# The second projections of both feed-forward stages: token tiles 0 and 2 by seven products per pair of k blocks, then tiles 1 and 3 as they were

## The reference, cut to what matters

```python
def _sqrelu_mlp(h, w1, w2):                 # h: 512 x 1024, w1: 1024 x 4096, w2: 4096 x 1024
    return jnp.square(jax.nn.relu(h @ w1)) @ w2
...
    for i in range(DEPTH_2):                # DEPTH_2 = 2
        ...                                 # attention, its residual sum and layer norm
        h = x * (1.0 + sc_c) + sh_c
        y = _sqrelu_mlp(h, mlp_w1[i], mlp_w2[i])
        x = _layer_norm(DN_ALPHA * x + (1.0 + g_c) * y, ln_g[i, 1], ln_b[i, 1])
```

## Time and profile before

| | |
|---|---|
| median of the runs | 3385.03 us |
| profiled execution, its own time | 3387.39 us |
| its span in the trace | 3385.8 us |
| mean granted TensorE clock | 0.97 |
| TensorE matmul busy | 3185.5 us (94%), 12406 records |
| VectorE busy | 1596.7 us (47%) |
| ScalarE, GpSimd busy | 563.2 us (17%), 250.1 us (7%) |
| HBM traffic, mean | 162 GB/s |
| first feed-forward stage, down projection | 2410.9 to 2633.5 us |
| second one | 3152.5 to 3372.4 us |

### The profile page before, as it was taken

The page is one execution under the profiler, slowest core; times in us unless marked ns, Lnnn a source line. Parts: engine busy times, 40 slices in busy tenths (PEclk is TensorE's granted clock), DMA queues, the critical chain, the costliest instruction groups (busy, mean ns, idle before and its releaser), DMA issues. The chain is left out here.

```text
span 3385.8 us, 38571 instructions
## 1 busy us (share of the span) xinstructions
PE 3185.5 (94%) x12406; PEld 1748.5 (52%) x12407; DVE 1596.7 (47%) x3615; ACT 563.2 (17%) x1280; POOL 250.1 (7%) x377
## 2 busy tenths in 40 slices
PE   7999999999989888979998998999999899899998
PEld 3446767744437433323333544488644566488543
DVE  6546576567656533324443577565202333465103
ACT  1002222210002111111221315310000233100000
POOL 1010000011110211112222100000000000000000
PEclk9999999999989899999999998999999999899999
DMA  7562121368762598997996611022121223022210
GB/s 236 169 199 63 38 75 38 88 210 260 245 215 102 206 362 338 360 362 289 358 346 218 202 69 38 31 94 100 75 99 37 75 75 131 25 94 83 92 75 25
DMA packets 252719, 524.45 MB, mean 155 GB/s; under 512 B 25977, under 2 KB 153588, under 8 KB 228026
## 3 DMA queue, kind: packets, MB, share of 16 engines
q1 hardware_dynamic: 204240, 380.16, 32.0%
q0 software_dynamic: 46992, 140.37, 12.2%
q10 hardware_dynamic: 1370, 2.37, 0.2%
HBM read 512.21 MB, written 36.77 MB: 162 GB/s over the span
## 5 line engine op out<-in xcount | busy, mean ns | idle before, releaser
L1334 PE MATMUL ps<-WR,hT 128*64 x832 | 384.9, 617 | 62.1 <-DVEq L2852 34.8
L1335 PE MATMUL ps<-WR,hT 128*64 128x512 f32 x832 | 384.9, 617 | 0.0
L1736 PE MATMUL ps<-WR 128*128 128x512 f32 x768 | 329.9, 592 | 0.0
L1334 PEld LDWEIGHTS ps<-WR,hT 128*64 128x64 f32 x832 | 117.1, 143 | 315.2 <-issue 315.2
L1736 PEld LDWEIGHTS ps<-WR 128*128 128x128 f32 x768 | 146.0, 190 | 182.8 <-issue 182.2
L2849 DVE COPY WR<-WR 128x1024 f32 x208 | 130.9, 691 | 227.3 <-SPq L640 175.0
L2612 DVE TENSOR_TENSOR WR<-ps,grow 128x1024 f32<-128x1024 f32 x20 | 24.5, 1223 | 439.2 <-PE ps L1747 368.5
L2301 DVE SCALAR_TENSOR_TENSOR WR<-xr,csil,WR 128x256 f32<-128x256 f32 x448 | 217.2, 485 | 16.0
L1015 PE MATMUL ps<-hT,WR 128*128 128x512 f32 x512 | 224.7, 592 | 0.0
L1697 PE MATMUL ps<-WR 128*128 128x256 f32 x960 | 217.0, 379 | 0.0
L1697 PEld LDWEIGHTS ps<-WR 128*128 128x128 f32 x960 | 182.4, 190 | 24.8
(11 more groups left out here) (409 smaller groups left out, 4581.2 us busy)
## 6 DMA issues: line engine op xcount, KB each, us to landing
WR<-in_w_gate SPq DMA_DIRECT2D x64, 1024.0 KB
WR<-in_w_up SPq DMA_DIRECT2D x64, 1024.0 KB
WR<-in_w_down SPq DMA_DIRECT2D x64, 1024.0 KB, 9.7
WR<-in_mlp_w SPq DMA_DIRECT2D x32, 2048.0 KB, 8.3
xr<-in_ada_w POOLq DMA_DIRECT2D x48, 1024.0 KB, 5.8
WR<-in_w_in SPq DMA_DIRECT2D x56, 512.0 KB, 6.6
xr<-in_w_ada POOLq DMA_DIRECT2D x16, 1024.0 KB, 5.8
WR<-in_w_in SPq DMA_DIRECT2D x16, 1024.0 KB, 6.5
```

The lines of the kernel that those rows point to most:

```text
L1334: mm(out[0:HALF], xT[u][:, k, 0:HALF], wa[:, :, k, :], start=(k == 0), stop=(k == KD - 1))
L1335: last = mm(out[HALF:P], xT[u][:, k, HALF:P], wb[:, :, k, :], start=(k == 0), stop=(k == KD - 1))
L1736: last = mm(ps[:, 2 * t + n, :], h1T[:, k, t * P:(t + 1) * P], w[:, k - 4 * u, 512 * n:512 * n + 512], start=(k == 0), stop=False)
```

## The change: what it does

The down projection of both stages is split into two phases.

Phase 1 makes token tiles 0 and 2 only. The 32 k blocks are taken as 16 pairs (k, k + 16). With tiles 0 and 2 as rows, the two blocks of a pair as the contraction and the two column halves of the output as columns, each pair is again a 2 x 2 block product. `down_pair` does it in seven products of 128x512 instead of eight. Each of the seven sums over all 16 pairs in its own PSUM bank (`DOWN_BANKS`; bank 7 stays free). VectorE makes the operands: `down_weight_sums` four 128x512 operations per pair, `row_sums` four 128x256 operations per two pairs. At the end `down_corners` turns the seven banks into the two tiles' outputs in SBUF (`down_c`), with seven 128x512 additions, after a copy of p1 by ScalarE.

Phase 2 makes tiles 1 and 3 by ordinary products in banks 6, 7, 4 and 5: eight fills of four k blocks, with four products per k block instead of eight. So all of `w2` is fetched twice: once in fills "seven" (two DMAs of 1 MB each), once in fills "down". Both take turns in slots 1, 2 and 3 only; slot 0 holds sums and outputs until tile 2 has been read by `residual`.

The residual sums and norms of stages 3 and 5 go over the tiles in the order 0, 2, 1, 3 (`TILES_OF`). In layer 0 the transposes of tiles 0 and 2 follow the second and third fill of phase 2; that of tile 1 stands ten matmuls into tile 3, and that of tile 3 at the end.

The diff, cut to its core:

```diff
+DOWN_BANKS = dict(p6=4, p5=0, p7=1, p4=2, p3=3, p1=6, p2=5)
+TILES_OF = {n: (0, 2, 1, 3) if n in (3, 5) else (0, 1, 2, 3) for n in range(6)}
...
-    ("down0", 1, [(1, 1), (3, 1), (2, 1), (0, 1), (3, 1), (2, 1), (1, 1), (0, 1)]),
+    ("seven0", 1, [(1, 2), (3, 2), (2, 2), (1, 2), (3, 2), (2, 2), (1, 2), (3, 2)]),
+    ("down0", 1, [(2, 1), (1, 1), (3, 1), (2, 1), (1, 1), (3, 1), (2, 1), (1, 1)]),
...
+            def down_pair(layer, k):
+
+                name = f"seven{layer}"
+                (b11, b12), (b21, b22) = weights_of(layer, k)
+                s1, s2, s3, s4 = [v[:, k % 2, :] for v in down_s[(k // 2) % 2]]
+                t1, t2, t3, t4 = down_t[k % 2]
+                a11, a12, a22 = [h1T[:, i, t * P:(t + 1) * P] for i, t in ((k, 0), (k + 16, 0), (k + 16, 2))]
+
+                def product(p, rows, weights):
+                    if k == 0:
+                        pe.wait_ge(*bank_read(layer, DOWN_BANKS[p], 7 * (UP_PAIRS - 1)))
+                    return mm(ps[:, DOWN_BANKS[p], :], rows, weights, start=(k == 0), stop=(k == 15))
+
+                if k % 2 == 0:
+                    have(name, k // 2)
+                    pe.wait_ge(*up_v(layer, f"s_{k // 2}"))
+                pe.wait_ge(*up_v(layer, f"t_{k}"))
+                product("p6", s2, t2)
+                product("p5", s1, t1)
+                product("p7", s3, t3)
...
+                product("p4", a22, t4)
+                product("p3", s4, b22).then_inc(sem("up_p"), 1)
+                last = product("p1", a11, b11)
...
+                last = product("p2", a12, b21)
+                if k % 2:
+                    spent(last, name, k // 2)
...
+                for k in range(16):
+                    down_pair(layer, k)
+                bank_free = {(1, 1): up_v(layer, f"c21_{UP_PAIRS - 1}"), (1, 0): up_a(layer, "p1_end"),
+                             (3, 0): up_v(layer, "u2_end"), (3, 1): up_v(layer, "c11_end")}
+                bank = {1: 6, 3: 4}
...
-                        for t in range(TT):
-                            for n in range(2):
+                        for t in (1, 3):
+                            for n in ((1, 0) if t == 1 else (0, 1)):
...
+            def row_sums(layer, j):
...
+                if j >= 2:
+                    dve.wait_ge(*up_p(layer, f"kp_{2 * j - 3}"))
+                link(V.tensor_tensor(s1, a(0, 2), a(1, 2), ALU.add))
+                link(V.tensor_tensor(s2, s1, a(0, 0), ALU.subtract))
+                link.mark(V.tensor_tensor(s3, a(0, 0), a(0, 2), ALU.subtract))
+                link(V.tensor_tensor(s4, a(1, 0), s2, ALU.subtract))
...
+            def down_weight_sums(layer, k):
...
+                if k % 2 == 0:
+                    dve.wait_ge(landed[ring.slot(name, k // 2)], ring.full(name, k // 2, 0))
+                if k >= 2:
+                    dve.wait_ge(*up_p(layer, f"kp_{k - 2}"))
+                link(V.tensor_tensor(t1, b12, b11, ALU.subtract))
+                link(V.tensor_tensor(t2, b22, t1, ALU.subtract))
+                link.mark(V.tensor_tensor(t3, b22, b12, ALU.subtract))
+                link(V.tensor_tensor(t4, b21, t2, ALU.subtract))
...
@@ corners(layer, i)
+                if i + 1 == UP_PAIRS:
+                    row_sums(layer, 0)
                 add(c12, "p3", c12)
...
@@ mlp(layer), VectorE
+                    else:
+                        down_weight_sums(layer, 0)
                     corners(layer, i)
-                dve.sem_inc(used[ring.slot(f"sums{layer}", 0)], 1)
+                down_weight_sums(layer, 1)
+                for j in range(1, 8):
+                    row_sums(layer, j)
+                    for k in (2 * j, 2 * j + 1):
+                        down_weight_sums(layer, k)
+                down_corners(layer)
```

More of the change, by code:

```diff
@@ L146 @@
 CORNERS = ("u2", "c11", "u4", "c22", "u3", "c12", "c21")
+DOWN_BANKS = dict(p6=4, p5=0, p7=1, p4=2, p3=3, p1=6, p2=5)
+TILES_OF = {n: (0, 2, 1, 3) if n in (3, 5) else (0, 1, 2, 3) for n in range(6)}
+RES_B = {0: 0, 2: TT, 3: 2 * TT, 4: 2 * TT + 2, 5: 3 * TT + 2}
+TURN_BANK = {n: (0, 6, 2, 4) if n == 4 else (0, 2, 4, 6) for n in range(6)}
 READ_BY = dict(p2="c11", p6="u2", p5="u4", p7="u3", p3="c12", p4="c21")
@@ L710, in mlp @@
                 for u in range(8):
+                    fill(f"seven{layer}", u, 0, *[(unit(f"seven{layer}", u, 2 * D * i, 2, D),
+                                                   mlp_w2[layer][:, 16 * i + 2 * u:16 * i + 2 * u + 2, :])
+                                                  for i in range(2)])
+                for u in range(8):
                     fill(f"down{layer}", u, 0, (unit(f"down{layer}", u, 0, 4, D),
@@ L1980, in norm_turn @@
             def norm_turn(n):
-                for t in range(TT):
+                for t in TILES_OF[n]:
                     normalize(n, t)
@@ L2608, in branch_in @@
                     if branch is None:
-                        dve.wait_ge(sem("res_b"), TT * (n - (n > 1)) + t + 1)
+                        at, tiles = 2 * t, TILES_OF[n]
+                        if n in (3, 5):
+                            at = {1: 6, 3: 4}.get(t)
+                            tiles = (1, 3)
+                        if t in tiles:
+                            dve.wait_ge(sem("res_b"), RES_B[n] + tiles.index(t) + 1)
+                            summed = ps[:, at:at + 2, :].rearrange("p b c -> p (b c)")
+                        else:
+                            summed = down_c[t // 2]
                         if t == TT - 1:
                             dve.sem_inc(used[ring.slot(*last_weights[n])], 1)
-                        link(V.tensor_tensor(scratch, ps[:, 2 * t:2 * t + 2, :].rearrange("p b c -> p (b c)"),
-                                             grow[:, :], ALU.mult))
+                        link(V.tensor_tensor(scratch, summed, grow[:, :], ALU.mult))
+                        if n in (3, 5) and t == 2:
+                            dve.sem_inc(used[ring.slot(f"sums{n // 2 - 1}", 0)], 1)
                     else:
@@ L2640, in residual @@
                 behind = 1 if branch is not None else 0
-                for t in range(TT + behind):
-                    if t < TT:
-                        branch_in(t)
-                    if sums is not None and t == TT - 1:
+                tiles = TILES_OF[n]
+                for i in range(TT + behind):
+                    if i < TT:
+                        branch_in(tiles[i])
+                    if sums is not None and i == TT - 1:
                         first_sums(sums)
-                    if t >= behind:
-                        gained(t - behind)
+                    if i >= behind:
+                        gained(tiles[i - behind])
             def weight_sums(layer, i):
@@ new lines, in down_corners, with add @@
+            def down_corners(layer):
+                name = f"seven{layer}"
+                (c11, c12), (c21, c22) = [[v[:, 512 * n:512 * n + 512] for n in range(2)] for v in down_c]
+                def add(into, p, to):
+                    V.tensor_tensor(into, ps[:, DOWN_BANKS[p], :], to, ALU.add).then_inc(sem("up_v"), 1)
+                dve.wait_ge(*up_a(layer, "p1_end"))
+                dve.wait_ge(*up_p(layer, "kp_15"))
+                add(c21, "p6", c11)
+                dve.wait_ge(*up_v(layer, "u2_end"))
+                dve.wait_ge(used[ring.slot(name, 7)], ring.free(name, 7, 0) + 1)
+                add(c11, "p2", c11)
+                add(c12, "p5", c21)
+                dve.wait_ge(*up_v(layer, "u4_end"))
+                add(c22, "p7", c12)
+                add(c21, "p7", c21)
+                dve.wait_ge(*up_v(layer, "u3_end"))
+                add(c12, "p3", c12)
+                add(c21, "p4", c21)
+                dve.wait_ge(*up_v(layer, "c21_end"))
```

79 lines of the change are left out of this document (52 added, 27 removed), and 2 rows, old and new, of the table STAGES.

## The result

| | before | changed |
|---|---|---|
| median | 3386.91 us (3384.12 to 3389.84, 4 runs) | 3353.49 us (3350.09 to 3358.51, 4 runs) |
| ratio, 95% interval | | 0.9902 [0.9889, 0.9915] |
| profiled execution, its span | 3385.8 us | 3348.8 us |

A forecast was written before the change was run, and what follows sets the result against it. The prediction took TensorE's own work to bound both down projections. Products -27.5 us and start waits +1.2 gave -26.3, so 3385.0 - 26.3 = 3358.7 us, with a range of 3354 to 3367 us.

The forecast's parts named there:

- The bound, TensorE's own work: Both down projections: TensorE's own work sets the time, so a removed product is worth its full step, 0.858 us.
- The products, -27.5 us: Down projections: 240 products in place of 256 per stage save 13.7 us per stage, 27.5 us in both.
- The start of phase 1, 0.6 us per stage: First weight load of phase 1 waits behind the first row sums: 0.6 us per stage, 1.2 us in both.
- VectorE's sums, hidden: Phase 1: VectorE's 3.8 us per pair, 60 us per stage, is hidden beside 96 us of products.
- The fills, nil: Phase 1 and 2 fills of 2 MB through three slots keep up with the products: no cost.
- Rival 3, the clock: Clock falls in phase 1: 3380 us at 0.90, 3434 at 0.72, slower than before; chance 0.04.
- The change of phase and the tails, nil: Banks 6, 4 and 5 are free in time for phase 2, and tile 3's end steps stay the same: nil.
- The attention between, nil: Attention between the feed-forward stages: its first fills may start later behind slot waits, at no cost.
- The range: Whole kernel: own range 3355 to 3362 us, including 2 us by which a median moves; 3354 to 3367 with small rivals.
- Theory B: From the experiments, not the prediction: the change also shortens the untouched front, by the layout of its instructions or queues.

The follow-up runs named there:

- e3: Also called the eighth product: changed kernel with an eighth, never read product per pair in phase 1, into bank 7; 3387.91 us, 1.0006 of the kernel before.
- e10: Changed kernel with p2 first instead of last in the first pair of k blocks of each stage; 3356.99 us, 0.9914 of the kernel before.
- e11: Changed kernel without the four row sums of the first two pairs (k = 0 and 1) of each stage; 3358.06 us, one run.
- e6: Changed kernel with VectorE making each weight sum of phase 1 twice; 3369.03 us, one run.
- e7: Changed kernel with phase 1 fills using two slots of the ring (1 and 3) in place of three; 3354.21 us, one run.
- e8: Changed kernel fetching only the first half of each phase 1 fill; 3355.25 us, one run.
- e4: Kernel with only the first feed-forward stage changed, the second as before; 3373.70 us, 0.9967 of the kernel before.
- e5: Kernel with only the second feed-forward stage changed, the first as before; 3371.97 us, 0.9953 of the kernel before.
- e1: Changed kernel run again with no edit; 3355.35 us, 0.9919 of the kernel before.

## Why the prediction was wrong, and where it was right

- **The bound, TensorE's own work.** Right: in both stages the chain is TensorE alone, before and after.
- **The products, -27.5 us.** Right, shown by the eighth product and by e10: 13.73 to 13.74 us per stage.
- **The start of phase 1, 0.6 us per stage.** Right in place, too large in size: 0.39 us, shown by e10 and e11. The sum had taken the delay of the weight load as the loss, at 0.6. The load was 0.50 us late (2401.72 in place of 2401.22, which is the 2401.60 at which the chain ends the up products less the 0.38 by which the load of the earlier trace rows leads the same point, 2411.08). Its record follows it by 0.03 us, where the earlier trace rows has 0.22, so the record itself was 0.31 late. The other 0.08 are in the first step: the row of 11 records lasts 4.96 us, where ten steps of 0.4292 and one record of 0.592 make 4.88. In the chain the same 0.39 stand as 0.15 between the up products and phase 1 and 0.24 in phase 1 itself (96.37 against 96.13).
- **VectorE's sums, hidden.** Right: e6 puts VectorE's round at 13.26 us for two pairs when doubled, and the undoubled one leaves TensorE no wait in phase 1. Its busy time rose by 120.3 us; 130 was the forecast.
- **The fills, nil.** Right: TensorE waits for none in the changed kernel, nor with two slots (e7), and half of the fetch less saves nothing (e8).
- **Rival 3, the clock.** It didn't come: 1.00 in phase 1 of both stages, with seven banks in turn. What the Trainium skill (TensorE: Matmul & The Clock Gate, "A second HAM failure mode: psum-queue depth-cycling") tells of banks in turn doesn't show here either.
- **The change of phase and the tails, nil.** Right: phase 2 follows phase 1 in the chain without a piece between, and the second stage's difference (-13.38) is that of the first.
- **The attention between, nil.** It was 0.8 us shorter in this pair. Over all traces it lies between 336.5 and 338.0 us, with 338.0 also in a changed kernel (e11). The piece that differs most, by 0.46 of the 0.79 us, is the first run of matmuls after the tail, before:

```profile
2644.91 16.82 PE ps L1507 x32
```

  and in the changed kernel:

```profile
2622.07 16.36 PE ps L1535 x32
```

  The clock is at its lower level (1.2 GHz, a granted clock of 0.50) after the tail, of whose 11.5 us TensorE was busy for some 2, and rises at another moment within this run. That this makes the 0.46 us is argued from the stretches and not tested. They are, before (PEclk is the third number from the end, ahead of DMA share and GB/s):

```profile
2645.00:2650.00 5.00, 5.00 (x6) 2.07 (x7) 2.16 (x2) 0.00 (x0) 2.41 (x5) 0.50 0.24 81
2650.00:2655.00 5.00, 5.00 (x12) 2.24 (x11) 0.00 (x0) 0.10 (x1) 0.59 (x1) 0.94 0.73 293
```

  and in the changed kernel:

```profile
2622.10:2627.00 4.90, 4.90 (x6) 2.13 (x7) 2.23 (x2) 0.00 (x0) 2.26 (x4) 0.51 0.21 74
2627.00:2632.00 5.00, 5.00 (x13) 2.26 (x12) 0.00 (x0) 0.40 (x1) 0.75 (x2) 1.00 0.97 264
```

- **The range: this is the step that failed.** The prediction put the scatter at "2 us by which a median moves", and had no other term for the parts outside the two stages. The three runs that it had of the kernel before lay within 4.7 us. The runs of the kernel before spread over 14 us, those of the changed one over 12.8 us (3350.1 to 3362.9, 15 runs). In the traces it is the front that scatters: 2217.6 to 2232.2 us over the thirteen, against 1.5 us in the attention between. From the standard deviations of single runs, 3.3 and 4.1 us, a median of four runs has, by my estimate, a standard error of some 2 us, so it can easily lie 4 us off; the range had half of that. The first comparison caught the changed kernel low (-33.4), with the short wait in its traced execution; the two repeats, at 3355.4 and 3356.6 us, lie in the range and near the forecast of 3358.7. Of the 5.2 us by which the result missed, 2.3 are this draw (3353.5 against a mean of 3355.8 for all 15 runs), 0.4 the start, 3.2 the open part below, less 0.7 because the forecast started from 3385.0 and the kernel before has a mean of 3385.7. Which side of the lower bound a median of four falls on is thus in part luck, for the result as for the two repeats.
- **What stays open.** All 58 runs of the kernel before have a mean of 3385.7, all 15 of the changed one 3355.8: -29.9 us with a standard error of 1.1. The two stages explain -26.7; with the attention's 0.8, which other traces don't repeat alike, it is -27.5. What is left, 2.4 to 3.2 us, is two to three standard errors, and the interval of the first comparison leaves 0.9919 out as well. Theory B in its full size is out: e3 keeps nearly all of the layout and came out above the kernel before, and e4 and e5 together gave -27. But the short wait at the adaptive-norm products is in five of the nine traces with both stages changed and in none of the four with a stage or both as before. Such a split comes by chance one time in ten (126 / 1287), and e1, e3, e10 and e11 have both stages changed and the long wait. So the change may make the short outcome more frequent; no run here shows it, or names a cause for one.

## What to carry to other kernels

Where the chain of waits is one engine alone, a product that goes is worth its step, and one trace prices it to 0.1 us. The scatter of the whole kernel is another matter: here it comes from the stages ahead, where TensorE waits for weights, and a range for the time must be made from many runs of the kernel before, not from three close ones. When two traces differ in a part that the edit doesn't touch, trace the same kernel again and compare the wait there, before looking for a cause in the edit. A scheme with fewer products and more sums pays as long as the sums of the next round fit in the products of this one with room for their signals; test that by doubling the sums, which shows at what length of VectorE's round TensorE begins to wait.

## What the runs showed of the hardware that was not expected

- A weight load that came 0.50 us late cost the stage 0.39 us (e10, e11): its record followed it by 0.03 us and not by 0.22, and the first step took 0.08 us longer. What brings the record closer to its load no run here shows.
- At the adaptive-norm products TensorE waited 12.1, 16.1 and 12.1 us for VectorE in three traces of the changed kernel, and over all thirteen traces 12.1 to 12.5 or 16.1 to 16.9 us, with nothing between. What decides it no run here shows.
- Two 1 MB fills at once moved up to 424 GB/s (40 slices of 2401 to 2498 us), beside VectorE at 56% and TensorE at a clock of 1.00, and neither got slower (0.430 us a record, 0.69 us a 128x512 sum, as in the earlier trace rows):

```profile
GB/s 51 385 422 7 7 27 372 417 49 0 37 377 424 27 0 24 405 421 15 0 51 399 416 0 0 32 410 414 15 0 66 358 412 32 0 90 392 382 2 0
```
